# Third mixer in a new order: the convolution first, the state-space heads in pairs around a projection each, top-k beside the gates, four decay rows

## The chip, the cores and the metric

One core of a Trainium2 chip runs the whole program. The time is device microseconds from the start to the end of one execution. The engines are TensorE (PE, with its weight loads PEld), VectorE (DVE), ScalarE (ACT), GpSimd (POOL) and SyncE (SP), which issues most of the DMAs. They run beside each other, each through its own instructions in order, and meet through semaphores.

## The reference, cut to what matters

256 tokens of width 1024 pass through two blocks. The first has two layers with three kinds of attention. The second has one layer: a mixer (the third mixer of the program) and a mixture of 32 experts, of which each token uses four. All is float32. The change touches the third mixer alone:

```python
h = _rms(x, norm_mix[l]) * (1.0 + sc_m) + sh_m
q, kv_lat, q_i, k_i, w_i, z, xbc, dt_raw, gate_logits = _split(h @ w_in[l])
q = _rms(q, q_norm[l]);  k, v = split(_rms(kv_lat, kv_norm[l]) @ w_kv_up[l]);  k = _rms(k, k_norm[l])
k_i = _layernorm_2(k_i, ...)
y_attn = _dsa_attention(q, k, v, q_i, w_i, k_i, rel_bias) @ w_attn_o[l]
y_ssd = _mamba2_ssd(z, xbc, dt_raw, ...) @ w_ssm_o[l]
mixed = sigmoid(g_attn) * y_attn + sigmoid(g_ssd) * y_ssd
x = x + g_m * (mixed @ w_out[l])
```

`_dsa_attention` gives each query a score per key from 8 index heads (the sum over heads of w_i * relu(q_i k_i)), keeps the best 64 keys and runs softmax attention over these, in 8 heads. `_mamba2_ssd` is a causal convolution of width 4 over 1536 channels, a SiLU, and then 16 heads: for each, a matrix of decays exp(acum_i - acum_j), times the product of C and B (`cb`), times dt, is applied to the values x. The result plus d_skip * x is gated by SiLU(z) and normed.

## The kernel before

Every engine's program is written out by hand, one after the other, in the file; the order of the lines of an engine is the order of its work. Activations lie feature-major: tile `hT` holds 8 chunks of 128 features by 256 tokens.

**PE.** `features` (line 439) makes one "projection": two chunks of 128 output features, each 8 matmuls over the contraction, in one PSUM bank. `take` hands out seven banks in rotation; a bank can be taken again once its reader has freed it, so the take of the n-th bank waits for the reader of the (n-7)-th. `weights` waits for one of four ring slots of 2 MB; SP fills them group after group in the list `groups`, each when PE has finished with the group four before. The 16 state-space heads go through `A{h}` (line 815, the cumulative decay of a head, spread over the rows), DVE's `decay_in`, an exponential on ACT, DVE's `decay_out`, and `ssm_values` (lines 479 and 480). The decay rows have two buffers in the tile `sc2` (named sc in the rows). Four heads share a bank `yssm`, which DVE reads with the skip term (line 1631).

The order of the mixer before: projections of q, kv, index queries, index key and index weights (lines 728 and 734); conv inputs x0 to x2; time steps (line 747) and two gates; the norms of q, kv and index key; key/value projection; index heads; then the transposes of x, and the loop over 16 heads, with six projections in three places (behind the decay rows of heads 2, 7 and 12); four gate projections; the norm sum of y (line 457); scores t0 to t7; turning of the softmax weights (line 473) and their values; the attention output `ya`, the state-space output `ys`, the last product `wo`.

**DVE** does the convolution as four taps over twelve chunks (line 1586 and the one before) once all conv inputs are there, then the index sums, the key norm, the decay work, the gate by z, and then top-k: eight rounds of max and replace on each half, the mask, and the addition to the bias rows `bm`, followed by the y norm and the score rows. **ACT** reads projections out of PSUM in the order of PE, and does all exponentials, Silu, Sigmoid and norms.

**The expert stage** begins when the mixer's result is normed and routed. Per expert 12 MB come in: four ring slots (line 1086) and two slots of the down weights, each issued by SP when PE has used what was in the slot.

## Time and profile before

| | us |
|---|---|
| median of 3 runs (lowest, highest) | 1880.21 (1879.91, 1883.44) |
| the profiled execution's own time | 1882.82 |
| its span, first to last instruction | 1881.0 |
| PE matmuls busy in the span | 1648.2 (88%) |
| DVE busy | 392.8 (21%) |
| ACT busy | 300.3 (16%) |
| chain that ended last | PE 68%, DMA 17%, DVE 7%, ACT 4% |

The span is cut into 40 slices of 47 us. The third mixer lies in slices 11 to 19; there the row of PE reads 7 9 9 5 7 6 8 6 9, the row of PEclk 8 9 9 7 7 7 8 7 9. From slice 22 to 39 the DMA rate is 427 to 429 GB/s. A matmul of float32 is two passes in the trace, so its counts (x128) are twice the number of matmuls in the code. The granted clock is given as a share of 2.4 GHz: 1.00 is 2.4 GHz, 0.50 is 1.2 GHz.

### The profile page before, as it was taken

To read this page: it belongs to the slowest core of one execution; us is meant where nothing else is said; L and a number is where in the kernel's file an instruction comes from. 1 tells how busy PE (TensorE), PEld (TensorE's weight loads), DVE (VectorE), ACT (ScalarE), POOL (GpSimd) and SP (SyncE) were. 2 spreads that over 40 slices of the span, in tenths; PEclk is the share of its full clock that TensorE was granted. 3 is DMA by queue.
4 is the path that set the end of the run, shared out by engine and by line. 5 is a ranking of instruction groups with operands and counts; after the bars stand their busy time and mean duration, and the time that the engine had idled before them with its cause. 6 is when DMAs were issued, how large, how long until landed. Compare 5 with 4: busy or idle time off the path is not lost.

```text
span 1881.0 us, 19486 instructions
## 1 busy us (share of the span) xinstructions
PE 1648.2 (88%) x7938; PEld 969.1 (52%) x7938; DVE 392.8 (21%) x881; ACT 300.3 (16%) x587; POOL 2.8 (0%) x9
## 2 busy tenths in 40 slices
PE   3998799988799576869799999999999999999996
PEld 3786577857687465758633343333333333333342
DVE  2103411071101623721211111111111111111111
ACT  2013311151302401220200110110101001010010
POOL 0000000000000000000000000000000000000000
PEclk7998899999899777879799999999999999999998
DMA  7347534482233112203499999999999999999994
GB/s 251 133 125 227 187 106 155 143 313 74 79 114 134 45 45 90 90 31 149 148 402 427 428 429 429 428 429 428 428 429 429 429 428 429 428 428 429 429 428 202
DMA packets 86184, 515.04 MB, mean 274 GB/s; under 512 B 7000, under 2 KB 10776, under 8 KB 61560
## 3 DMA queue, kind: packets, MB, share of 16 engines
q1 hardware_dynamic: 82328, 513.43, 67.9%
q10 hardware_dynamic: 3632, 0.54, 0.2%
q8 instruction: 35, 0.57, 0.1%
q0 software_dynamic: 176, 0.39, 0.1%
q14 instruction: 13, 0.11, 0.0%
HBM read 511.20 MB, written 3.15 MB: 273 GB/s over the span
## 4 chain that ended last, share of the span: by engine, by line
PE 68%; DMA 17%; DVE 7%; ACT 4%; issue 2%; ACTq 1%; DVEq 0%; SPq 0%
PE psum L439 25%; PE psum L930 18%; DMA ring<-in_w_gu 15%; PE psum L999 8%; PE psum L903 3%; PE psum L448 3%; PE psum L479 2%; PE psum L913 2%; DMA ring<-in_w_ada 2%; PE psum L921 1%; DMA w_router<-in_w_router 1%; DVE sc L1405 1%; PE psum L496 1%; PE psum L815 1%; PE psum L480 1%
## 5 line engine op out<-in xcount | busy, mean ns | idle before, releaser
L930 PE MATMUL psum<-ring,hg 128*64 128x512 f32 x2048 | 458.6, 596 | 21.4 <-DMA ring<-in_w_gu 21.4
L439 PE MATMUL psum<-hT,ring 128*128 128x256 f32 x1504 | 342.4, 391 | 6.2 <-ACT hT L1190 6.2
L439 PEld LDWEIGHTS psum<-hT,ring 128*128 128x128 f32 x1504 | 296.0, 197 | 52.5 <-issue 9.9
L930 PEld LDWEIGHTS psum<-ring,hg 128*64 128x64 f32 x2048 | 139.2, 137 | 312.4 <-issue 267.7
L999 PE MATMUL psum<-w_down,hiddenT 128*64 128x512 f32 x1024 | 229.3, 600 | 28.2 <-ACT hiddenT L1365 25.2
L999 PEld LDWEIGHTS psum<-w_down,hiddenT 128*64 128x64 f32 x1024 | 74.9, 138 | 162.2 <-issue 162.2
L1767 DVE TENSOR_SCALAR gu<-psum 128x512 f32<-128x512 f32 x32 | 22.1, 692 | 529.2 <-PE psum L930 529.2
L1361 ACT ACTIVATE hidden<-gu 128x512 f32<-128x512 f32 x32 | 20.2, 630 | 316.2 <-DVE gu L1767 316.2
L439 PE MATMUL psum<-yT,ring 128*128 128x256 f32 x256 | 60.9, 403 | 9.3 <-DVE yT L1397 9.3
L903 PE MATMUL psum<-pick,h_tok 128*128 128x128 f32 x512 | 63.5, 284 | 2.9 <-DVE passes L1750 2.9
L903 PEld LDWEIGHTS psum<-pick,h_tok 128*128 128x128 f32 x512 | 60.5, 197 | 8.2 <-issue 8.2
L913 PE MATMUL psum<-putT,o_slot 64*128 64x256 f32 x512 | 63.9, 389 | 0.7 <-ACT o_slot L1368 0.7
L913 PEld LDWEIGHTS psum<-putT,o_slot 64*128 64x128 f32 x512 | 46.8, 186 | 31.0 <-issue 25.2
L439 PEld LDWEIGHTS psum<-yT,ring 128*128 128x128 f32 x256 | 52.1, 204 | 18.9 <-DVE yT L1397 11.0
L1368 ACT ACTIVATE o_slot<-psum 128x512 f32<-128x512 f32 x32 | 19.1, 597 | 237.7 <-PE psum L999 237.7
L448 PE MATMUL psum<-ring,hT 128*128 128x512 f32 (+2 forms) x192 | 56.3, 451 | 0.0
L1739 DVE COPY bias_row<-k_all 128x128 f32 (+1 forms) x32 | 7.2, 224 | 210.2 <-PE psum L937 210.1
L448 PEld LDWEIGHTS psum<-ring,hT 128*128 128x128 f32 x192 | 36.5, 190 | 18.0 <-issue 14.3
L479 PE MATMUL psum<-sc 128*64 128x256 f32 x32 | 15.6, 594 | 29.7 <-DVE sc L1405 29.7
L921 PE MATMUL psum<-b_gu,bias_row 64*128 64x512 f32 x128 | 36.1, 641 | 0.0
L1359 ACT ACTIVATE putT<-psum 128x256 f32<-128x256 f32 x32 | 12.3, 384 | 144.8 <-PE psum L937 144.8
L1182 ACT ACTIVATE wide<-xT 128x512 f32<-128x512 f32 x20 | 11.7, 625 | 141.4 <-DVE xT L1427 72.2
(348 smaller groups left out, 1283.8 us busy)
## 6 DMA issues: line engine op xcount, KB each, us to landing
ring<-in_w_gu SPq DMA_DIRECT2D x128, 2048.0 KB, 22.5
w_down<-in_w_dn SPq DMA_DIRECT2D x64, 2048.0 KB, 20.7
ring<-in_w_in SPq DMA_DIRECT2D x24, 2048.0 KB, 8.0
ring<-in_w_ada SPq DMA_DIRECT2D x12, 2048.0 KB, 10.6
ring<-in_w_out SPq DMA_DIRECT2D x6, 2048.0 KB, 9.9
ring<-in_w_in SPq DMA_DIRECT2D x2, 2064.0 KB, 7.8
ring<-in_w_ssm_o SPq DMA_DIRECT2D x2, 2048.0 KB, 7.8
ring<-in_w_in SPq DMA_DIRECT2D x1, 2112.0 KB, 8.1
```

The costliest lines, as they stand in the source:

```text
L439: mm = pe.matmul(bank[0:m, c * T:(c + 1) * T], w[:, k, c0 + c * P:c0 + c * P + m], src[:, k, :], start=(k == 0), stop=(k == k_n - 1))
L448: mm = pe.matmul(bank[:, 0:n], src[:, k, blk * P:(blk + 1) * P], w[:, k, c0:c0 + n], start=(k == 0), stop=(k == k_n - 1))
L479: pe.matmul(bank[rows, c * T:(c + 1) * T], v[:, 0, cols], wT[:, 0:T], start=True, stop=False)
L480: return pe.matmul(bank[rows, c * T + P:(c + 1) * T], v[:, 1, cols], wT[:, T:W3], start=False, stop=True)
L903: mm = pe.matmul(psum[:, 4 + part, j * P:j * P + width * CAP], h_tok[:, b, c * P:(c + 1) * P], pick[:, b, 0:width, :], start=(b == 0), sto ...
L913: mm = pe.matmul(psum[:, c // 2, c % 2 * T:(c % 2 + 1) * T], o_slot[r, i * P:(i + 1) * P], putT[r, side, :], start=False, stop=False, skip ...
L921: pe.matmul(psum[:, 4 + part, :], bias_row[r, side, :, :].rearrange("p h s -> p (h s)"), b_gu[r, :], start=True, stop=False, skip_group_ch ...
L930: mm = pe.matmul(psum[half * CAP:(half + 1) * CAP, 4 + part, :], hg[:, k, side, :], w[:, c0:c0 + 512], start=False, stop=(k == KC - 1), sk ...
L999: mm = pe.matmul(psum[half * CAP:(half + 1) * CAP, 7, :], hiddenT[:, i, j * CAP:(j + 1) * CAP], w_down[:, j, c0:c0 + 512], start=(k == 0), ...
L1361: act.activation(hidden[:, 0, :], gu[:, 0, :], ACT.Sigmoid, scale=1.702).then_inc(ev("g_sig"), 1)
L1368: act.activation(o_slot[:, :], psum[:, 7, :], ACT.Copy).then_inc(ev("o_slot"), 1)
L1767: dve.tensor_scalar(gu[:, 0, :], psum[:, 4, :], 7.0, None, ALU.min).then_inc(ev("g_in"), 1)
```

## The change

Nothing is computed otherwise; the third mixer's work is put in another order on every engine.

- The weight groups, and with them the projections, begin with the conv inputs, time steps and two gates. The convolution is done two chunks at a time on DVE, right behind each projection, with its SiLU on ACT.
- The loop over 16 heads becomes a loop over 8 pairs. In a pair PE issues both decay rows, one projection (q, q, kv, index queries twice, index key with index weights, z0, z1), then the values of the pair before. DVE does the two `decay_in`, a small norm (`aside`), the two `decay_out` of the pair before.
- The decay rows have four buffers, in the tile `idx`, instead of two in `sc2`.
- The index heads, the key/value projection and the score rows stand between the projections of z and of the gates; so DVE's top-k lies beside the gate projections. The key norm stands ahead of top-k, the y norm behind the scores.
- The state-space output comes ahead of the attention output, with the turning and the values of the attention between its four projections.
- SP issues the bias rows behind x2 instead of x0, and `ao` behind `so0` and `so1`.

```diff
-    decay = early[:, NB * D:NB * D + 2 * W3].rearrange("p (i n) -> p i n", i=2)
...
+    decay = idx
...
-    for name, a0, a1 in [("q2", 0, 512), ("kvqi", 512, 1024), ("qkwi", 1024, 1352),
-                         ("x0", 2376, 2888), ("x1", 2888, 3400), ("x2", 3400, 3912), ("dtg", 3912, 4440),
+    for name, a0, a1 in [("x0", 2376, 2888), ("x1", 2888, 3400), ("x2", 3400, 3912), ("dtg", 3912, 4440),
+                         ("q2", 0, 512), ("kvqi", 512, 1024), ("qkwi", 1024, 1352),
                          ("z0", 1352, 1864), ("z1", 1864, 2376),
                          ("g1", 4440, 4952), ("g2", 4952, 5464), ("g3", 5464, 5976)]:
-        if name == "z0":
+        if name == "g1":
             group("kvup", a["w_kv_up_2"][0], 0, 1024)
         group(name, a["w_in_2"][0], a0, a1)
-    group("ao", a["w_attn_o_2"][0], 0, 1024)
     for j in range(2):
         group(f"so{j}", a["w_ssm_o_2"][0], 512 * j, 512 * j + 512)
+    group("ao", a["w_attn_o_2"][0], 0, 1024)
...
-                              decay[:, h % 2, :], h % 2)
+                              decay[:, h % 4, :], h % 2)
...
-        for h in range(SH):
-
-            bank = take(f"A{h}")
-            for b in range(NB):
-                mm = pe.matmul(bank[:, b * P:(b + 1) * P], dta[:, b, h:h + 1].broadcast_to([P, P]), up,
-                               start=True, stop=True)
-            full(mm, f"A{h}")
-            if h % 5 == 2 and h // 5 < 3:
-
-                for i in range(2):
-                    project_aside(2 * (h // 5) + i)
-            if h >= 1:
-                ssm_values(h - 1)
-        ssm_values(SH - 1)
...
+        def project_aside(p):
+
+            if p < 2:
+                w = weights("q2")
+                features(f"q2.{p}", w, hT, 256 * p, 2)
+                if p:
+                    last_of("q2", "q2.1")
+            elif p < 4:
+                w = weights("kvqi")
+                features(("kvl", "qi0")[p - 2], w, hT, 256 * (p - 2), 2)
+                if p == 3:
+                    last_of("kvqi", "qi0")
+                    pe.wait_ge(ev("sq_q"), 1)
+                    for j in range(2):
+                        square_sums(j, "q2ms", slice(2 * j, 2 * j + 2))
+            elif p == 4:
+                features("qi1", weights("qkwi"), hT, 0, 2)
+                pe.wait_ge(ev("sq_kv"), 1)
+                sum_chunks("kvms", wide, [range(4, 6)], means[:, 2, :])
+            elif p == 5:
+                w = weights("qkwi")
+                bank = take("ki")
+                for half in range(2):
+                    for k in range(KC):
+                        mm = pe.matmul(bank[half * HEAD:(half + 1) * HEAD, 0:T], w[:, k, 256:320], hT[:, k, :],
+                                       start=(k == 0), stop=(k == KC - 1))
+                full(mm, "ki")
+                bank = take("wi")
+                for b in range(NB):
+                    for k in range(KC):
+                        mm = pe.matmul(bank[:, b * AH:(b + 1) * AH], hT[:, k, b * P:(b + 1) * P], w[:, k, 320:328],
+                                       start=(k == 0), stop=(k == KC - 1))
+                full(mm, "wi")
+                last_of("qkwi", "wi")
+            else:
+                features(f"z{p - 6}", weights("z0"), hT, 256 * (p - 6), 2)
+                if p == 6:
+                    read_out(pe, "ki")
+                    bank = take("kimean")
+                    mm = pe.matmul(bank[:, 0:T], K["half"][:, :], ki[:, :], start=True, stop=True)
+                    full(mm, "kimean")
+                else:
+                    last_of("z0", "z1")
+                    pe.wait_ge(ev("sq_ki"), 1)
+                    bank = take("kivar")
+                    mm = pe.matmul(bank[:, 0:T], K["half"][:, :], wide[:, 6, :], start=True, stop=True)
+                    full(mm, "kivar")
+        for p in range(SH // 2 + 1):
+            if p < SH // 2:
+                for h in (2 * p, 2 * p + 1):
+                    bank = take(f"A{h}")
+                    for b in range(NB):
+                        mm = pe.matmul(bank[:, b * P:(b + 1) * P], dta[:, b, h:h + 1].broadcast_to([P, P]), up,
+                                       start=True, stop=True)
+                    full(mm, f"A{h}")
+                project_aside(p)
+            if p == 1:
+                read_out(pe, "xt11")
+            if p >= 1:
+                for h in (2 * p - 2, 2 * p - 1):
+                    ssm_values(h)
+
+        w = weights("z1")
+        features("z2", w, hT, 0, 2)
+        pe.wait_ge(ev("ki"), 1)
...
+        for h in range(4):
+            index_rows(h)
+        features("z3", w, hT, 256, 2)
+        last_of("z1", "z3")
+        for h in range(4, AH):
+            index_rows(h)
+        w = weights("kvup")
+        pe.wait_ge(ev("kvl"), 2)
+        for j in range(2):
+            features(f"k2.{j}", w, kvl, 256 * j, 2)
+        for b in range(NB):
+            tokens(f"v2.{b}", w, kvl, b, 512, 512)
+        last_of("kvup", "v2.1")
+        w = weights("g1")
+        features("g2", w, hT, 0, 2)
+        pe.wait_ge(ev("sq_k"), 1)
+        for j in range(2):
+            square_sums(j, "k2ms", slice(2 * j, 2 * j + 2))
+        features("g3", w, hT, 256, 2)
+        last_of("g1", "g3")
+        w = weights("g2")
+        features("g4", w, hT, 0, 2)
+        pe.wait_ge(ev("qk2"), 2)
+        for h in range(4):
+            head_rows(f"t{h}", q2, h // 2, k2, h // 2, h % 2)
+        features("g5", w, hT, 256, 2)
+        last_of("g2", "g5")
+        for h in range(4, AH):
+            head_rows(f"t{h}", q2, h // 2, k2, h // 2, h % 2)
         pe.wait_ge(ev("sq_y"), 1)
         sum_chunks("yms", wide, [range(4), range(4, 8)], means[:, 3, :])
...
+        pe.wait_ge(ev("y_ssm"), 1)
+        for j in range(2):
+            w = weights(f"so{j}")
+            for i in range(2):
+                features(f"ys{2 * j + i}", w, yS, 256 * i, 2)
+                if (j, i) != (0, 0):
+                    h = 4 * j + 2 * i - 2
+                    if h > 0:
+                        value_2(h - 2)
+                        value_2(h - 1)
+                    turn_2(h)
+                    turn_2(h + 1)
+            last_of(f"so{j}", f"ys{2 * j + 1}")
+        value_2(4)
+        value_2(5)
+        turn_2(6)
+        turn_2(7)
+        value_2(6)
+        value_2(7)
...
-            if name == "x0":
+            if name == "x2":
...
+        for i in range(6):
+            read_out(dve, f"xbc{i}")
+            for k in range(4):
+                for j in range(2):
+                    c = 2 * i + j
+                    x = xbc[:, c, k:k + T]
+                    if k == 0:
+                        ins = dve.tensor_scalar(xbcs[:, c, :], x, vec("conv_w", c), None, ALU.mult)
+                    else:
+                        dve.wait_ge(ev("tap"), 6 * i + 2 * k - 1 + j)
+                        ins = dve.scalar_tensor_tensor(xbcs[:, c, :], x, vec("conv_w", 12 * k + c), xbcs[:, c, :],
+                                                       ALU.mult, ALU.add)
+                    ins.then_inc(ev("conv") if k == 3 else ev("tap"), 1)
...
+        def aside(p):
+
+            if p == 4:
+                dve.wait_ge(ev("rstd_q"), 2)
+                stt(flat(q2), flat(q2), vec("q_norm_2"), flat(wide[:, 0:4, :]), ALU.mult, ALU.mult, ev("qk2"))
+            if p == 5:
+                dve.wait_ge(ev("rstd_kv"), 1)
+                for c in range(2):
+                    stt(kvl[:, c, :], kvl[:, c, :], vec("kv_norm", c), stat[:, :], ALU.mult, ALU.mult, ev("kvl"))
+            if p == 7:
+                ch.free(dve.tensor_tensor(ki[:, :], ki[:, :], product(dve, "kimean")[:, 0:T], ALU.subtract), "kimean")
+                ch.after(dve.tensor_copy(sink[:, :], ki[:, 0:1]), ev("ki_centred"))
...
-            A, d = product(dve, f"A{h}"), decay[:, h % 2, :]
-            if h >= 2:
-                dve.wait_ge(*values_done[("ssm", h - 2)])
+            A, d = product(dve, f"A{h}"), decay[:, h % 4, :]
...
+        for p in range(SH // 2 + 1):
+            if p < SH // 2:
+                decay_in(2 * p)
+                decay_in(2 * p + 1)
+                aside(p)
+            if p >= 1:
+                decay_out(2 * p - 2)
+                decay_out(2 * p - 1)
...
+        dve.wait_ge(ev("rstd_k"), 2)
+        stt(flat(k2), flat(k2), vec("k_norm_2"), flat(wide[:, 0:4, :]), ALU.mult, ALU.mult, ev("qk2"))
```

How the instructions stand on PE in the loop. `dta` gives the decay rows, `hT,ring` is a projection, `sc` (before) and `idx` (after) with the values are a head's values. Before, from the decay rows of head 2 to those of head 4:

```order
L815 MATMUL psum<-k_all,dta 128x128 x2
L439 MATMUL psum<-hT,ring 128x256 x32
L479 MATMUL psum<-sc 64x256
L480 MATMUL psum<-sc 64x128
L815 MATMUL psum<-k_all,dta 128x128 x2
L479 MATMUL psum<-sc 64x256
L480 MATMUL psum<-sc 64x128
L815 MATMUL psum<-k_all,dta 128x128 x2
```

After, pairs 1 and 2 of the loop:

```order
L802 MATMUL psum<-k_all,dta 128x128 x4
L439 MATMUL psum<-hT,ring 128x256 x16
L479 MATMUL psum<-idx,sc 64x256
L480 MATMUL psum<-idx,sc 64x128
L479 MATMUL psum<-idx,sc 64x256
L480 MATMUL psum<-idx,sc 64x128
L802 MATMUL psum<-k_all,dta 128x128 x4
L439 MATMUL psum<-hT,ring 128x256 x16
```

Before, only three of the sixteen heads had projections (two at once) between decay rows and values; now every pair has one of 16 matmuls there.

On DVE around top-k, where `xbc<-xbc,zg` is the gate by z, `k<-k,vecs,wide` the key norm and `top` the first of the eight rounds. Before:

```order
L1631 SCALAR_TENSOR_TENSOR xbc<-xbcs,d_skip,psum 128x256 x2
L1397 TENSOR_TENSOR xbc<-xbc,zg 128x2048
L1397 TENSOR_TENSOR idx<-idx,k_all 128x384
L1657 COPY idx<-idx 128x384
L1661 MAX top<-idx 128x8
```

After:

```order
L1475 SCALAR_TENSOR_TENSOR idx<-idx,wi 128x256
L1467 TENSOR_TENSOR xbc<-xbc,zg 128x2048
L1475 SCALAR_TENSOR_TENSOR k<-k,vecs,wide 128x1024
L1467 TENSOR_TENSOR idx<-idx,k_all 128x384
L1739 COPY idx<-idx 128x384
L1743 MAX top<-idx 128x8
```

The index sums now stand directly ahead of the gate by z and of top-k, and the key norm has moved in between; before, the whole loop over the heads lay between the index sums and top-k.

## Rows read from the trace of the kernel before

**Rows 1.** Windows: us; busy us (instructions) of PE, PEld, DVE, ACT, POOL; clock; DMA
```profile
489.40:599.40 110.00, 109.99 (x513) 94.90 (x514) 2.40 (x11) 14.44 (x28) 0.00 (x0) 0.94 0.31 106
599.40:645.80 46.40, 24.77 (x102) 16.88 (x100) 30.42 (x76) 27.81 (x47) 0.00 (x0) 0.74 0.26 91
645.80:757.70 111.90, 82.13 (x321) 62.57 (x321) 35.59 (x102) 14.69 (x25) 0.00 (x0) 0.73 0.16 57
...
790.80:813.40 22.60, 4.59 (x34) 3.33 (x33) 12.95 (x23) 8.43 (x34) 0.00 (x0) 0.61 0.17 64
813.40:898.20 84.80, 82.43 (x377) 68.53 (x378) 15.64 (x32) 8.29 (x14) 0.00 (x0) 0.96 0.27 100
...
1234.00:1850.00 616.00, 568.57 (x2890) 225.85 (x2890) 86.40 (x185) 57.22 (x104) 0.00 (x0) 1.00 1.01 428
```

**Rows 2.** Waits of SP's queue from 900 us: total us, times, longest
```profile
SPq L1086 <- PE psum L930: 446.3, 124, 30.1
```

**Rows 3.** Timeline of SP: start, us, what is issued
```profile
938.76 11.81 SPq L1086 DMA_DIRECT2D ring<-in_w_gu  x4
```

**Rows 4.** Chain that ended last, at expert 0: start, us, what
```profile
934.98 3.58 PE psum L930 x16
```

**Rows 5.** Chain that ended last, third mixer: start, us, what
```profile
489.41 37.68 PE psum L439 x160
...
527.09 6.25 PE psum L728 x32
533.33 4.22 PE psum L734 x32
...
581.89 3.48 PE psum L747 x32
585.37 13.92 PE psum L439 x64
...
653.51 14.97 PE psum L439 x64
...
787.46 3.47 PE psum L457 x16
...
827.01 41.69 PE psum L439 x192
```

**Rows 6.** The same chain, small matmuls at full clock and the first turned weights
```profile
668.49 0.58 PE psum L479 x2
669.06 0.22 PE psum L480 x2
669.28 0.66 PE psum L815 x4
...
813.38 1.62 PE psum L473 x6
...
820.39 0.48 PE psum L473 x3
```

**Rows 7.** DVE by form, 643 to 790 us: busy, mean ns, idle before and its end
```profile
L1405 DVE SCALAR_TENSOR_TENSOR sc<-sc,dt,cbs 128x256 f32<-128x256 f32 x16 | 7.8, 485 | 0.6
...
L1405 DVE SCALAR_TENSOR_TENSOR sc<-psum,neg_acum,k_all 128x128 f32<-128x128 f32 x16 | 5.6, 351 | 57.1 <-PE psum L815 56.7
...
L1631 DVE SCALAR_TENSOR_TENSOR xbc<-xbcs,d_skip,psum 128x256 f32<-128x256 f32 x8 | 3.8, 481 | 17.4 <-PE psum L480 17.2
```

**Rows 8.** Timeline of PE: a head's values, and the idle time before
```profile
672.64 1.00 PE L479 MATMUL psum<-sc 128*64 128x256 f32 x2 [2.72 <-DVE sc L1405]
```

**Rows 9.** Timeline of DVE: top-k's first row, the bias add behind it, the scores
```profile
761.20 0.56 DVE L1397 TENSOR_TENSOR idx<-idx,k_all 128x384 f32<-128x384 f32 x1
...
780.75 3.36 DVE L1397 TENSOR_TENSOR bm<-bm,idx 128x3072 f32<-128x3072 f32 x1
...
796.57 3.52 DVE L1678 SCALAR_TENSOR_TENSOR sc<-psum,bm 128x384 f32<-128x384 f32 x6
```

**Rows 10.** Windows again: the stretch right behind the index weights
```profile
537.50:543.00 5.50, 5.50 (x14) 4.42 (x14) 0.00 (x0) 0.18 (x1) 0.00 (x0) 0.50 0.78 271
```

287 lines of the change are left out of this document (117 added, 170 removed).

## The prediction

> **What bounds the kernel now.** I read the windows view of the third mixer first, then the chain of waits, then the waits of SP's queue and of the engines, and the timelines of VectorE (DVE), ScalarE (ACT) and TensorE (PE) where the change moves work.
>
> The third mixer runs from 489.4 to 898.2 us, 408.8 us. From 489.4 to 599.4 PE is busy all the time, from 813.4 to 898.2 nearly. Between, it is busy 24.8 of 46.4 us, 82.1 of 111.9 and, ahead of the softmax weights, 4.6 of 22.6, at a granted clock of 0.74, 0.73 and 0.61 [rows 1]. The busy time there is itself long, because much of it was done at the lower of the two clock levels, 1.2 GHz (0.50), instead of 2.4 GHz. So the mixer is bound by chains between PE, DVE and ACT in the middle and by PE at both ends.
>
> Does the end move with the mixer? From 1234 to 1850 us the expert stage is bound by its weights: the 16 DMA engines are full (428 GB/s) [rows 1]. But this stream has its start from PE: SP's issues of expert weights waited 446.3 us for PE's expert matmuls [rows 2], and the second expert's first load left at 938.76 [rows 3], just when PE had used the first quarter of expert 0 (934.98 + 3.58) [rows 4]. All bytes behind that point are the same, and everything from 898.2 to 938.8 hangs on the mixer's last product. A microsecond gained in the mixer is therefore a microsecond at the end.
>
> **What PE has to do in the mixer.** The change takes nothing away from PE; it puts the same matmuls in another order. So I add up the work at the full clock.
> - A "projection" of two 128-feature chunks is 16 matmuls of 256 columns. Six take 41.69 us at clock 1.0, 6.95 each or 0.434 per matmul [rows 5]. There are 31 of them (q 2, kv and index queries 3, conv inputs 6, gates 8, z 4, ys 4, wo 4); the four half-size ones of the attention output and the key/value projection add 3. 34 x 6.95 = 236.3 us.
> - Index key 6.25, index weights 4.22, time steps 3.48 [rows 5]: 13.95 us.
> - Sums of squares: 3.47 for the state-space norm [rows 5]; four of 512 columns (2 x 0.434) and four of 256: 8.7 us in all.
> - Cumulative decay of a head (line 815) 0.66, its values (lines 479 and 480) 0.58 + 0.22 = 0.80, at full clock [rows 6]. Sixteen heads: 23.4 us.
> - Index rows and score rows, 8 heads each: 384 columns, 1.5 x 0.434 = 0.65. 10.4 us.
> - Turning the weights 8 x 0.48 (line 473) [rows 6] and 8 x 0.80 for the values: 10.2 us.
> - Sixteen transposes of x at 0.16 (a third of 0.48), two cb products at 0.65, three small ones: 4.0 us.
>
> Sum 307.0 us. To it come the clock's losses and the waits that remain.
>
> **Clock.** The mixer still starts slow after the norm: 5 projections took 37.68 us instead of 34.75 [rows 5], 2.9 us. In the window after the 8-column index weights PE was at 0.50 for 5.5 us without a pause [rows 10]; a matmul pass took 0.39 us there (14 in 5.5) against 0.22 at full clock, so about 2.7 us are lost. The index weights are now in pair 5 of the loop, with values and decay rows behind them; I charge 2.7 again. Together 5.6 us.
>
> **The convolution first.** DVE's taps were 48 in one piece, with PE idle behind them. Now they go chunk pair by chunk pair: about 3 us of DVE under each projection of 6.95, and ACT's read (0.6) and two Silu there too. The last chunk pair ends some 5 us after x2 while PE has 3.48 + 13.9 us of time steps and gates. The softplus chain hides there as well. Cost 0; without that cover 5 us, once.
>
> **The loop in pairs.** Before, a head between projections went through DVE, ACT, DVE and PE one after the other: PE waited 2.72 us for the decay [rows 8] and did its part at half clock, and the stretch of [rows 1], 111.9 us, less its 6 projections leaves 70.2 us for 16 heads, 4.4 each, where PE's own work at full clock is 1.46. DVE idled 57.1 us in total for line 815 and 17.4 for the values [rows 7]. Now PE issues both decay rows of a pair (1.3), a projection (6.95), then the values of the pair before (1.6): 9.9 us. DVE has, per pair, two decay_in (three operations of 0.35 and a one-column copy, about 1.35 with gaps), two decay_out (0.49 for 256 columns and about 0.35 for 128, 0.9 with gaps), every second pair the skip term (2 x 0.48) [rows 7], and for some the q, kv or index-key norm of 0.6 to 1.3: 4.5 to 6.6 us. DVE waits for the values' bank at the end of every second pair, so decay_in of the next starts about 1.1 us late; its decay_out must be there 8.3 us after PE's pair start and comes at about 5.6 (6.6 in pair 5). Four decay buffers make the wait for the values two pairs old. ACT's exponentials lie half a projection ahead. I charge no wait. If the cover failed, a pair would pay up to the old price of 2 x (4.4 - 1.46) = 5.9 us. The two copies of the index-key chain (kimean in pair 6, kivar in pair 7) have a projection between them for 1.2 us of DVE and ACT; cost 0.
>
> **Top-k beside the gates.** Let 0 be the loop's last value. PE: z2 6.95, four index heads 2.6, z3 6.95, four more 2.6, key/value 6.95, g2 6.95, two sums 1.7: 34.7. DVE's index sums are inside that. ACT does its two Ln/Exp pairs until about 36.6, DVE the key norm (1.28) until 38. Top-k and the bias add, from 761.20 to 784.11, take 22.9 us [rows 9]: 61. The first score (3.52 us for six, 0.59) frees its bank at 61.6. PE meanwhile does g3, g4 (13.9), t0 to t3 (2.6), g5 (6.95), t4, t5 (1.3) and reaches t6 at 59.5; seven banks rotate, and t6 wants that of t0. **PE waits 2.2 us.** Before, the same place cost 22.6 us with 4.6 busy [rows 1], as nothing else was left to do. Behind it, from the first score (796.57 [rows 9]) to the first weights turned (813.38 [rows 6]) it was 16.8 us: scores, maxima, exponentials, the sums' reciprocal. So these are ready at 61 + 16.8 = 77.8, and the y norm, which stands ahead of the reciprocal, before that. PE needs y at 80.3 (t6, t7, sums, g6, g7) and the weights at 94.2 (two ys projections later). Both are covered, by 2.5 us at the least and by 16; a top-k that is late by x costs x. Turning and values are interleaved with ys; two waits stay, for the last read of o2 (0.8) and for the mix of the last product (1.6). Waits together 4.6 us.
>
> **The queue of SP.** The bias rows are now issued behind x2, where SP waits for the last layer's h_ready; behind it stands dtg, needed 45 us later. Each later weight group has its slot freed 15 us or more before it is read, and a load lands in about 8 us. Cost 0. ACT loads its tables once less.
>
> **Sum.** 307.0 + 5.6 + 4.6 = 317.2 us in place of 408.8: 91.6 us less. The profiled execution took 1882.82 us (span 1881.0), so 1791.2; the median of the runs shown is 2.6 lower, 1880.21, which makes **1788.6, say 1789 us**.
>
> **Unknown costs, from both sides.** The row of a clock drop in the small matmuls of a pair or in the transposes ahead of the loop does not exist in this form. Lower end: no drop anywhere, not even behind the index weights, and no wait at t6: 5 us less, 1784. Upper end: one drop like that of [rows 10] per pair, 2.7 x 8 = 21.6 us, 1811. I take none, since within the old loop values and decay rows straight after a projection ran at full clock ([rows 6] are those) and since behind the 16-column time steps, 3.48 us long, two projections took 13.92 us, full clock [rows 5].
>
> The Trainium skill ("TensorE: Matmul & The Clock Gate", section "A second HAM failure mode: psum-queue depth-cycling") speaks against the change: a kernel that cycles through its PSUM banks can pause so often between groups that the clock goes back and forth. The case here cycles seven banks, with groups of 1.3, 6.95 and 1.6 us. By that rule the loop would lose its drop per pair (the rival below); by the rows it loses one.
>
> **Rivals.**
> 1. *The clock falls in most pairs.* For: it fell in [rows 10] while PE was busy without a pause. Against: the groups between projections are 2.9 us, those there 4.22 behind 6.25. 21.6 us: about 1810.
> 2. *A wait in the chains that I hid*: ACT serves reads and exponentials in one queue, and the Silu of z stands ahead of the key norm; or DVE's bank waits meet PE in the loop. 10 us (a late top-k of 7 and 0.4 per pair): about 1799.
> 3. *The end does not follow the mixer*, because the expert stream is bound by something before its start that doesn't move. Against: [rows 2 to 4]. Then 1880.
> 4. *Slower: PE works at 1.2 GHz for most of the mixer.* One mechanism: small groups and short waits keep the granted clock down over projections that had 1.0. With a share s of the time at half clock and a matmul 1.8 times as long there, 307 / (1 - 0.45 s) + 4.6. It decides from s = 0.54, about the 0.73 that the old loop shows [rows 1]. At a clock of 0.70 (s = 0.6): 425, so 1897. Against: in the old loop two projections behind a stretch at half clock took 14.97 us [rows 5], only 1.1 over full clock.
>
> **How the numbers follow.** My forecast (1784 to 1796) 0.55; rival 1 0.16; rival 2 0.22; rival 3 0.03; rival 4 0.03; the rest is a better clock than charged. The range takes in rivals 1 and 2: 1782 to 1812. What a measurement of this kernel can tell from no change is about 0.2%, 3.8 us. Faster 0.95, same 0.02, slower 0.03.
>
> **What would show it.** The mixer's last product should end near 806 us of the span in place of 898.2; PE busy over 95% from 489 to 806; a granted clock of 0.95 or more there; one PE wait of about 2 us for DVE's first score row; the pairs of the loop 10 us apart; DVE's first top-k instruction about 38 us behind the last head's values; and the same 428 GB/s at the end. I am wrong if PE waits for the decay in the loop, if a clock of 0.50 appears inside it more than once, or if the wait ahead of the scores is over 5 us.

## The result, and the profile after

The changed kernel takes 1779.49 us (median of 4 runs, 1777.62 to 1782.28); beside it the kernel before took 1881.83 (4 runs, 1879.91 to 1884.57). The ratio is 0.9456, 95% interval 0.9437 to 0.9475. The forecast was 1789, its range 1782 to 1812: the sign and the place were right, the gain was larger than forecast (102.3 us in place of 91.6), and the time lies 2.5 us below the range. The profiled execution took 1779.8 us, its span is 1777.7.

First the windows of the changed kernel, as in [rows 1]: stretch, then busy time and instructions of PE, PEld, DVE, ACT, POOL, then PE's granted clock, DMA share, GB/s. The first is the whole third mixer, the second the loop of head pairs.

```profile
487.60:794.30 306.70, 299.62 (x1487) 252.65 (x1488) 121.90 (x309) 81.39 (x153) 0.00 (x0) 0.97 0.31 111
554.20:633.60 79.40, 78.98 (x421) 64.69 (x420) 38.18 (x107) 19.64 (x36) 0.00 (x0) 0.96 0.24 81
...
612.00:617.50 5.50, 5.50 (x20) 4.75 (x20) 4.08 (x12) 1.04 (x2) 0.00 (x0) 0.60 0.97 365
...
690.00:702.00 12.00, 8.52 (x35) 6.82 (x34) 11.19 (x13) 2.75 (x4) 0.00 (x0) 0.86 0.48 176
...
900.00:1600.00 700.00, 654.36 (x3338) 261.37 (x3336) 100.03 (x218) 66.67 (x121) 0.00 (x0) 1.00 1.01 428
```

The mixer's projections begin at 487.65 and its last product is done at 794.32: 306.7 us in place of 408.8 (489.4 to 898.2, [rows 1]), 102.1 less. PE is busy 97.7% of it at a clock of 0.97. Behind it the two kernels need the same: 983.4 us to the end of the span here, 982.8 before. The expert stream still moves 428 GB/s.

SP's queue and the chain at expert 0 answer to [rows 2 to 4]: the wait in total, the first load of expert 1, and the PE piece that released it (830.98 + 3.58 = 834.56).

```profile
SPq L1135 <- PE psum L979: 447.4, 124, 29.9
```

```profile
834.76 8.40 SPq L1135 DMA_DIRECT2D ring<-in_w_gu  x3
```

```profile
830.98 3.58 PE psum L979 x16
```

Where did PE's 79.4 us in the loop go? The chain that ended last (start, us, what) shows one pair from values to values, then the decay rows and the projection of pair 6, right behind the index weights of pair 5, then the index rows of four heads. L439 is a projection, L479 and L480 are the values, L802 the decay rows.

```profile
570.79 6.91 PE psum L439 x32
577.70 0.59 PE psum L479 x4
578.29 0.22 PE psum L480 x4
578.51 1.09 PE psum L802 x8
579.60 6.91 PE psum L439 x32
...
611.64 2.01 PE psum L802 x8
613.65 8.34 PE psum L439 x32
...
640.70 0.43 PE psum L819 x4
641.13 0.43 PE psum L820 x4
641.57 0.32 PE psum L819 x4
641.88 0.43 PE psum L820 x4
```

A pair is 570.79 to 579.60, 8.80 us, without a gap. The values of **both** heads take 0.59 + 0.22 = 0.81 us, what one head took in [rows 6]. The index rows of four heads take 1.61 us, 0.40 each, where 384 columns alone would be 0.65. DVE's idle time for the decay rows is down from 57.1 us [rows 7] to 22.8, and now costs nothing, as PE does not wait for it:

```profile
L1475 DVE SCALAR_TENSOR_TENSOR idx<-psum,neg_acum,k_all 128x128 f32<-128x128 f32 x16 | 5.6, 351 | 22.8 <-PE psum L802 22.4
```

The waits of PE in the mixer (total us, times, longest); left out are one ahead of its first product, 0.8 us without a releaser and two of 0.2 for the skip terms. The timeline shows the largest, which stands where [rows 1] had 22.6 us with 4.6 busy, and the chain the sum of squares behind it:

```profile
PE psum L465 <- DVE sc L1755: 3.5, 1, 3.5
...
PE psum L439 <- DVE zg L1467: 1.6, 1, 1.6
...
PE psum L479 <- ACT probT L1182: 0.8, 2, 0.4
```

```profile
693.62 0.48 PE L465 MATMUL psum<-k,q 64*128 64x128 f32 x2 [3.48 <-DVE sc L1755]
```

```profile
695.22 5.21 PE psum L457 x16
```

There is no wait for a decay. One wait of 3.5 us for the first score is there, and the sum of squares behind it takes 5.21 us instead of 3.47 [rows 5], at a clock of 0.86 in its window.

### The profile page after: what moved, and what is told of

Its sections match the earlier page's. It is cut to its first block, busy times and chain, and to the rows that moved or that the text cites. A ratio compares the mean times of both kernels' runs of the same rounds, so it can differ in the third digit from the quotient of the medians.

```text
span 1777.7 us, 19486 instructions
## 1 busy us (share of the span) xinstructions
PE 1608.0 (90%) x7938; PEld 945.4 (53%) x7938; DVE 393.0 (22%) x881; ACT 299.6 (17%) x586; POOL 2.8 (0%) x9
## 4 chain that ended last, share of the span: by engine, by line
PE 70%; DMA 18%; DVE 6%; ACT 3%; issue 1%; ACTq 1%; SPq 0%; DVEq 0%
PE psum L439 25%; PE psum L979 19%; DMA ring<-in_w_gu 16%; PE psum L1048 9%; PE psum L952 4%; PE psum L448 3%; PE psum L962 2%; DMA ring<-in_w_ada 2%; PE psum L970 1%; DMA w_router<-in_w_router 1%; PE psum L479 1%; PE psum L496 1%; ACT hiddenT L1435 1%; ACT hg L1424 0%; PE psum L473 0%
## 5 line engine op out<-in xcount | busy, mean ns | idle before, releaser
L439 PE MATMUL psum<-hT,ring 128*128 128x256 f32 x1504 | 337.1, 386 | 6.4 <-ACT hT L1239 6.2
L439 PEld LDWEIGHTS psum<-hT,ring 128*128 128x128 f32 x1504 | 290.4, 194 | 52.0 <-issue 11.7
L439 PE MATMUL psum<-yT,ring 128*128 128x256 f32 x256 | 60.7, 403 | 9.3 <-DVE yT L1467 9.3
L439 PEld LDWEIGHTS psum<-yT,ring 128*128 128x128 f32 x256 | 52.0, 204 | 18.9 <-DVE yT L1467 11.0
L448 PE MATMUL psum<-ring,hT 128*128 128x512 f32 (+2 forms) x192 | 56.3, 451 | 0.0
L448 PEld LDWEIGHTS psum<-ring,hT 128*128 128x128 f32 x192 | 36.5, 190 | 18.0 <-issue 14.3
L1424 ACT ACTIVATE hg<-psum 128x512 f32<-128x512 f32 x32 | 19.1, 597 | 89.4 <-PE psum L952 89.4
L1858 DVE TENSOR_TENSOR hidden<-hidden 128x512 f32<-128x512 f32 x32 | 33.4, 1045 | 1.1
## 6 DMA issues: line engine op xcount, KB each, us to landing
ring<-in_w_ada SPq DMA_DIRECT2D x12, 2048.0 KB, 10.5
```

Source lines behind the costliest of these rows:

```text
L439: mm = pe.matmul(bank[0:m, c * T:(c + 1) * T], w[:, k, c0 + c * P:c0 + c * P + m], src[:, k, :], start=(k == 0), stop=(k == k_n - 1))
L448: mm = pe.matmul(bank[:, 0:n], src[:, k, blk * P:(blk + 1) * P], w[:, k, c0:c0 + n], start=(k == 0), stop=(k == k_n - 1))
L1424: act.activation(hg[:, 4 * part:4 * part + 4, 0:width, :], bank[:, :, 0:width, :], ACT.Copy)\
L1858: dve.tensor_tensor(hidden[:, 2, :].rearrange("s (i p) -> s p i", i=4), apart(hidden[:, 1, :]), apart(hidden[:, 0, :]), ALU.mult).then_inc ...
```

## Experiments

Twelve kernels in three series, each series on one chip beside 9 runs of the kernel before (1881.60 to 1881.75 in the median). "Mixer" is the stretch from the first projection to the last product, read from the chain that ended last: 306.7 us in the changed kernel, and in its second run below.

### Values of a pair apart

```diff
                     full(mm, f"A{h}")
+                    if p >= 2 and h == 2 * p:
+                        ssm_values(2 * p - 3)
                 project_aside(p)
...
-                for h in (2 * p - 2, 2 * p - 1):
-                    ssm_values(h)
+                ssm_values(2 * p - 2)
```

> The changed kernel with the two heads of a pair no longer neighbours when their values are computed: one decay row stands between them (the values of head 2p-3 come between the decay rows of heads 2p and 2p+1). The work is the same. Theory A: the two heads of a pair write different halves of the output rows, and PE does their values side by side when they follow each other: 0.81 us for both in the changed kernel's chain, where I had charged 0.80 for each. Apart, six or seven pairs pay up to 0.8 us more, the overlap with the decay row gives some back: mixer 3 to 6 us longer. Theory B: the values are only quick because nothing makes PE wait for them, and the 0.80 of the old row held some waiting: then no difference (under 1 us).

1785.41 us, ratio 0.9484 (0.9471 to 0.9497); mixer 313.3, 6.6 longer. Its chain:

```profile
571.55 6.91 PE psum L439 x32
578.46 0.58 PE psum L479 x2
579.03 0.22 PE psum L480 x2
579.25 0.64 PE psum L802 x4
...
581.33 6.91 PE psum L439 x32
```

Apart, each head costs 0.80 again, and the two decay rows 1.28 instead of 1.09; the pair takes 9.78 us instead of 8.80. No wait appears. The same instructions are dearer when the two heads are not neighbours.

### Neighbours on the same half

```diff
+        def in_order(h):
+            return h // 4 * 4 + (0, 2, 1, 3)[h % 4]
...
-            mm = apply_values(psum[:, banks[name][0], :], h // 2 % 2, x_tok, slice(h * HEAD, (h + 1) * HEAD),
-                              decay[:, h % 4, :], h % 2)
+            mm = apply_values(psum[:, banks[name][0], :], hh // 2 % 2, x_tok, slice(hh * HEAD, (hh + 1) * HEAD),
+                              decay[:, h % 4, :], hh % 2)
```

> The changed kernel with the state-space heads taken in the order 0, 2, 1, 3 of each four, on TensorE, VectorE and ScalarE alike: the two heads of a pair then write the same 64 partitions of their bank, where they wrote different ones. Number, shapes and order of the instructions are those of the changed kernel. Theory A (the values of two heads run side by side because they write different halves): the four products of a pair take 1.5 to 1.6 us instead of 0.81, the pair 9.5 to 9.6 instead of 8.80, and over 8 pairs the kernel is 5 to 6.5 us slower, 1784 to 1785.5. Theory B (the values are short when they stand together behind a projection, whatever they write, and the single heads' 0.80 us was a cost of going back and forth between shapes): the pair stays at 8.80 us and the time at 1778.5.

1783.14 us, ratio 0.9477 (0.9464 to 0.9490), in a series of its own; mixer 310.1, 3.4 longer. A pair's values in its chain:

```profile
578.49 0.58 PE psum L479 x2
579.07 0.22 PE psum L480 x2
579.28 0.43 PE psum L479 x2
579.72 0.22 PE psum L480 x2
```

The four pieces are 1.44 us (578.49 to 579.93) in place of 0.81, and the pair is 9.44 (571.58 to 581.02) in place of 8.80. The instructions stand in the same order, with the same shapes; only the place they write differs. In the changed kernel a pair writes the same columns of the bank in different 64 partitions, here neighbouring columns in the same 64. That is theory A: two heads run side by side when they write different halves. Of the 5.1 us that eight pairs would give, 1.4 came back in pair 6, whose projection took 6.91 here and 8.34 there; why the clock was back earlier is open.

The index rows are the same question with the rows *read* in place of the partitions written:

```diff
-        for h in range(4):
+        for h in (0, 2, 1, 3):
             index_rows(h)
...
-        for h in range(4, AH):
+        for h in (4, 6, 5, 7):
```

> On TensorE, the index score rows are issued in the order of heads 0, 2, 1, 3, then 4, 6, 5, 7, so that two neighbours read the same 64 rows of the array, where the changed kernel alternates between the lower and the upper 64. Theory A (two heads on different halves run side by side, and that is why four heads take 1.61 us where I had charged 0.65 each): the four heads take 2.0 to 2.6 us, 0.43 to 1 more per group of four. Theory B (their matmuls are only short, whatever half they read): 1.6 us per group as before. The time of the kernel moves by no more than 2 us either way, which this single look does not resolve; the rows of the chain decide.

A single run, 1782.23 us, so the rows decide and not the time; mixer 309.4. The first and the last piece of four heads in its chain:

```profile
640.53 0.41 PE psum L819 x2
...
642.36 0.43 PE psum L820 x2
```

From 640.53 to 642.79 they take 2.26 us in place of 1.61. In the order 0, 1, 2, 3 there are three neighbours on different halves, here one (2 and 1). Four heads alone would be 4 x 0.65 = 2.60; 2.60 - 1.61 is 0.33 for each of three, and 2.60 - 0.33 = 2.27 for one. So each pair of neighbours on different halves saves a third of a microsecond, half a head. Twice 0.65 is 1.3 of the 2.7 us that the mixer is longer; the wait for the first score is 3.5 us as before, and the rest lies behind it, where the last rows and the sum of squares (5.94) ran slower than in the changed kernel.

### Projections ahead of the loop

The eight projections of the loop, and what ACT and DVE do for them, stand ahead of it, so nothing lies between a pair's decay rows and its values.

```diff
+        for p in range(SH // 2):
+            project_aside(p)
+
         pe.wait_ge(ev("dta"), 1)
         bank = take("acum")
...
                     full(mm, f"A{h}")
-                project_aside(p)
```

> The changed kernel with the eight projections of the loop (q, kv, index queries, index key and weights, z0, z1) and their reads and norms moved ahead of the loop; pairs and four decay rows stay. Theory A (the projections beside the loop give the gain, since they cover DVE and ACT): the loop is bound by DVE, about 2.7 + 1.8 + 0.5 us a pair, some 5.2 us against the 1.9 us that PE needs: 8 x 3.3 = 26 us longer, and the projections ahead cost the same 62 us as before. Some more for the clock, which falls in the loop and must come back behind it (1 to 3 us). Theory B (pairs and four rows are what removes the old loop's chain, the projections' place matters little): under 10 us longer.

1819.08 us, ratio 0.9671 (0.9656 to 0.9685); the span is 39.2 us longer. One pair of its chain:

```profile
646.02 1.12 PE psum L479 x2
...
648.47 1.17 PE psum L805 x4
649.71 0.36 DVE idx L1477
...
652.93 0.36 DVE idx L1477
653.33 1.11 PE psum L479 x2
```

PE does the values and the first decay row at half clock, then DVE forms two exponents and the first decay, then PE again: 7.31 us a pair, where the changed kernel pays 8.80 - 6.91 = 1.89 beside its projection. So the cover is worth 5.4 us a pair, and that price holds the lower clock too (0.59 from 640 to 660 us). I had expected less for this run since I took DVE's work alone for the bound; but PE's decay rows stand behind its values, so PE and DVE take turns. The prediction's own price of a failed cover, 5.9, was the better one.

### Single heads

Two decay rows instead of four; each head's decay row, half a projection, then the values of the head before.

```diff
-                              decay[:, h % 4, :], h % 2)
+                              decay[:, h % 2, :], h % 2)
...
-            if h >= 4:
-                dve.wait_ge(*values_done[("ssm", h - 4)])
+            if h >= 2:
+                dve.wait_ge(*values_done[("ssm", h - 2)])
```

> The changed kernel with single heads instead of pairs, two decay rows instead of four, and half a projection (8 matmuls) beside each head; at head 8 the values come ahead of the half projection, which banks demand. Theory A: half a projection, 3.46 us, is long enough to cover decay_in and decay_out (2.3 us after the decay row), so the chain stays hidden; what is lost is the pairing of values and decay rows on PE (0.4 + 0.1 us a head, 6 to 8 us) and one wait of 2 us at head 8: 7 to 11 us longer. Theory B: pairs and four rows are needed to hide the chain: each head shows a wait of about 1 us or more, and the whole is 20 us or more longer.

1792.63 us, ratio 0.9523 (0.9509 to 0.9538); span 13.4 longer. A head of its chain (L448 is the projection, L489 the values' first piece; 0.22 of L490 and the decay row's 0.64 follow):

```profile
562.58 3.46 PE psum L448 x16
566.03 0.58 PE psum L489 x2
...
567.47 3.46 PE psum L448 x16
```

No wait: half a projection beside each head, 3.46 us, already hides the chain. A head takes 4.90, two 9.80, 1.0 more than a pair; over eight that is 8 of the 13. The rest are waits: 2.4 us at head 8, and 1.3 and 1.2 for the skip terms behind the values of heads 7 and 11, where the changed kernel has 0.2 each. Behind the first two the clock fell and cost another 3 us (5.67 us for half a projection); about as much was saved behind the index weights, where it did not fall (see below). So what the pair has over single heads is for the larger part not a better cover but that its two heads are neighbours on PE.

### Convolution in one piece

```diff
-        for i in range(6):
-            read_out(dve, f"xbc{i}")
-            for k in range(4):
-                for j in range(2):
-                    c = 2 * i + j
+        read_out(dve, "xbc5")
+        for k in range(4):
+            for c in range(12):
```

ACT's Silus stand behind its last read accordingly.

> The changed kernel with the convolution in one piece again, behind the last conv input: 48 taps on DVE, 17.6 us, then the chain of the time steps. The prediction said that the new place costs nothing since it is covered. Theory A: DVE is done with the taps at 532.8 + 17.6 = 550.4, the softplus chain takes some 4 us more, so PE, which is ready at 549.6 for it, waits until about 555 and loses some clock: 5 to 9 us longer. Theory B: the order of time steps and taps gives PE enough to do: under 1 us.

1788.83 us, ratio 0.9514 (0.9500 to 0.9529); mixer 316.1, 9.4 longer. PE's first piece behind the convolution, and the transposes:

```profile
555.10 1.04 PE psum L727 x4
...
556.56 3.49 PE psum L735 x16
```

PE idles 6.6 us for dta, and the sums and transposes behind it then take 1.04 and 3.49 us where the changed kernel has 0.35 and 1.79: 2.4 us of lower clock, 3.0 with the products ahead of the loop. I had priced the missing cover at 5 us in the prediction; it is 9. (Behind the index weights this kernel lost 1.6 us less than the changed one: 7.23 us for the projection there in place of 8.34, and 1.18 for the values in place of 1.49. No run says why.)

### Half the top-k ahead of the gate

```diff
-        dve.wait_ge(ev("z_gate"), 1)
-        tt(yS[:, :, :], yS[:, :, :], zg[:, :, :], ALU.mult, ev("y_gated"))
-        dve.wait_ge(ev("rstd_k"), 2)
-        stt(flat(k2), flat(k2), vec("k_norm_2"), flat(wide[:, 0:4, :]), ALU.mult, ALU.mult, ev("qk2"))
...
         for cols, q in PARTS:
+            if q:
+                dve.wait_ge(ev("z_gate"), 1)
+                tt(yS[:, :, :], yS[:, :, :], zg[:, :, :], ALU.mult, ev("y_gated"))
+                dve.wait_ge(ev("rstd_k"), 2)
+                stt(flat(k2), flat(k2), vec("k_norm_2"), flat(wide[:, 0:4, :]), ALU.mult, ALU.mult, ev("qk2"))
             work, best = idx[:, 1, cols], top8[:, q, :]
```

The changed kernel once more, in the same series:

> The changed kernel once more, in the same series as the three edits of it that follow, so that their times can be set beside it. Every theory: 1779.5 us within 2.

1778.50 us (1777.65 to 1779.46), ratio 0.9454 (0.9441 to 0.9467), mixer 306.7.

> On VectorE, the addition of the causal mask, the copy and the first half of the top-k stand ahead of the product with the z gate and the normalization of the keys, which now stand between the two halves. Nothing else changes. In the changed kernel TensorE idles 3.5 us at head 3's score row, because its bank frees only when VectorE has cleared it behind both halves, and the sum of squares behind that wait takes 5.21 us where it took 3.47 before. Theory A (the wait is a plain chain on VectorE, and the clock fall behind it is the wait's): the score banks are cleared about 11 us earlier, the wait goes, the sum of squares is back at 3.5 us, and the mixer and the kernel end 5 us earlier (3.5 + 1.7), at about 1774. Theory B (the normalized keys are then what comes late: the score rows wait for them instead, which are written 11.4 us later): the keys are needed at about 683 us, and the half takes 11.4 us from 670, so they would be ready at about 684: a wait of 1 to 3 us at the first score row, and the time is 1776 to 1779. Theory C (the fall of the clock has nothing to do with the wait): the wait goes, the sum keeps its 5.2 us, 1776.

1771.99 us (1769.15 to 1773.63), ratio 0.9416 (0.9403 to 0.9429); once more in the next series 1771.06 (1769.60 to 1774.22), ratio 0.9415 (0.9402 to 0.9428):

> The kernel with the first half of the top-k ahead of the gate once more, as the base of the two edits of the index weights that follow in this series: 1772 us within 2, by every theory.

The mixer takes 300.8 us, 5.9 less. The chain where the wait was:

```profile
691.84 0.43 PE psum L466 x4
692.27 3.65 PE psum L457 x16
```

The wait is gone, the sum of squares is back at 3.65, and no new wait for the keys comes in: theory A. The expectation names head 3; by the rotation of seven banks the row that waited in the changed kernel is that of t6, the seventh bank taken behind that of t0. This version beats both kernels. Its two profiles also need 1.9 and 2.2 us less behind the mixer than the changed kernel's in the same series (980.9 and 980.6 against 982.8), and begin the mixer 2.4 and 1.2 us later, which the edit does not explain. Behind the mixer the largest piece is this: the first down projection of expert 0 took 9.48 us in the changed kernel, at the lower clock, and 7.09 here, as all later ones do. In both kernels and in the profiles of the ten other edits and reruns the clock was lower there: 8.42 to 9.78 us for that piece, behind much the same short waits of the routing (2.0 and 2.9 us in the changed kernel, 2.3 and 2.6 in the two of this version); no run says why it was not in the two of this version.

### The clock behind the index weights

Block 0 of the 8-column products ahead of the index key:

```diff
+                for b in range(NB):
+                    for k in range(KC):
+                        mm = pe.matmul(wi_bank[:, b * AH:(b + 1) * AH], hT[:, k, b * P:(b + 1) * P],
+                                       w[:, k, 320:328], start=(k == 0), stop=(k == KC - 1))
+                    if b == 0:
+                        bank = take("ki")
...
```

> On TensorE, the sixteen 8-column products of the index weights for block 0 stand ahead of the index key's products, those for block 1 behind them, where the changed kernel has all 32 in a row. The changed kernel shows the clock at half speed for about 5.5 us from 606 us on, and the work behind the row (decay rows 1.06, values 2.01, a projection 8.34 instead of 6.91) loses 3.0 us. Theory A (the run of narrow products is what the clock falls for): in two pieces of 1.9 us each between full work the clock stays at 1.00, and the kernel is up to 3 us faster, 1776 to 1778. Theory B (it falls after any narrow products, or for another reason): the clock falls as before or twice, 1779 to 1783.

1778.74 us, ratio 0.9456 (0.9444 to 0.9469): no change. The two rows of 16 passes and the key between them:

```profile
598.69 1.92 PE psum L773 x16
600.61 7.91 PE psum L779 x32
608.52 1.88 PE psum L773 x16
```

The clock now fell twice (0.72 from 600 to 606 us, 0.74 from 612 to 618): the key (7.91 in place of 6.29) pays what the values and decay rows behind the second row no longer pay. Next, on top of the early half of the top-k, the narrow products one by one between those of the key, and then all but two of them left out:

```diff
                         mm = pe.matmul(bank[half * HEAD:(half + 1) * HEAD, 0:T], w[:, k, 256:320], hT[:, k, :],
                                        start=(k == 0), stop=(k == KC - 1))
+                        mm = pe.matmul(wi_bank[:, half * AH:(half + 1) * AH], hT[:, k, half * P:(half + 1) * P],
+                                       w[:, k, 320:328], start=(k == 0), stop=(k == KC - 1))
```

> Beside the early half of the top-k, the 32 products of the index weights stand one by one between the 32 of the index key, so that no two narrow products are neighbours. When they stood in two pieces of 16 the clock still fell, behind the first piece of 1.9 us, and nothing was won. Theory A (a run of narrow products is what the clock falls for): alternating, it stays at 1.00, and the kernel is up to 3 us faster than the one without, about 1769; the whole group takes at least 6.29 + 3.87 = 10.2 us as before, less if a narrow one hides beside a wide one. Theory B (the share of narrow products over a stretch is what counts, not that they are neighbours): the clock falls in the group or behind it, which then takes up to 13 us, and the time is 1771 to 1775.

> Beside the early half of the top-k, of the 32 products of the index weights only the first of each block is left (the index weights are then sums over the first 128 of 1024 features; everything else is computed). Their row takes 3.87 us, at 0.12 each. Theory A (the narrow products make the clock fall): the row shrinks to 0.24 us, the half speed behind it goes, and the kernel is 3.6 + 3.0 = 6.6 us faster, about 1765.5. Theory B (the clock falls there for another reason, such as the index key's 64-column products ahead): the row goes and the fall stays, 3.6 us faster at most, 1768 to 1769.

These two texts count passes: what they call 32 products are 16 matmuls, 32 passes in the trace, and the last edit leaves 2 of the 16: it leaves out the sums over the other 896 of 1024 features.

Interleaved: 1775.24 us, ratio 0.9439 (0.9426 to 0.9452), mixer 301.9, 1.1 longer than without; the other 3 us lie behind the mixer, where the first down projection took 9.78 us. With two products: 1768.15, ratio 0.9399 (0.9386 to 0.9412), mixer 294.4, 6.4 shorter. Windows of the interleaved group, and of the stretch behind the two products:

```profile
598.70:613.30 14.60, 14.44 (x67) 7.91 (x68) 5.19 (x15) 1.28 (x3) 0.00 (x0) 1.00 0.00 1
```

```profile
606.00:618.00 12.00, 11.79 (x72) 9.83 (x72) 5.45 (x16) 2.10 (x5) 0.00 (x0) 1.00 0.51 175
```

Both hold a clock of 1.00 where the changed kernel shows 0.60 from 612 to 617.5 (its windows above). So the row of narrow products, during which PE counts as busy, has a part in the fall, here as in [rows 10]: taken out or pulled apart, it leaves the clock at 1.00. But the row alone does not make the clock fall. In the single heads' kernel the same 32 passes stand in one row (L792); ahead of them, where the changed kernel has the key, are a head's values and a decay row (L815):

```profile
617.57 0.64 PE psum L815 x4
618.21 3.47 PE psum L792 x32
621.68 0.58 PE psum L489 x2
```

The row takes 3.47 us instead of 3.88, the values behind it are at full speed, and the granted clock is 1.00 from 618 to 624. The 32 passes of 16 columns of the time steps, 3.48 us at 532.23, are followed by full clock as well (13.91 us for two projections). So what the fall needs beside the row, what stands ahead of it or the moment at which it comes, stays open. Alternating also changes two things at once, the neighbours of a narrow product and the time over which the narrow ones are spread.

Alternating saves the 3.0 us but makes the group 14.3 us instead of 6.29 + 3.88: one wide and one narrow product take 0.90 instead of 0.64. If all of that is put on the narrow one, a pass of it costs 0.25 instead of 0.12. In the other edit the two products that stay take 0.54 us in place of 3.88: 3.3 for the row and 3.0 for the clock, 6.4 measured in the mixer. 3.5 of it were lost again behind the mixer, most of it at the routing and expert 0, which ran at the lower clock (first gather 6.54 against 5.32, first down projection 8.42 against 7.09), so the kernel is only 2.9 us faster.

## What the prediction had right, and the step that failed

**The bound and the end.** Right. The mixer's microseconds arrive at the end one for one: 102.1 in the mixer, 102.3 in the medians. Rival 3 is out.

**No wait in the loop.** Right: 79.0 of 79.4 us busy. The run with the projections ahead shows what the cover is worth (5.4 us a pair, 40.6 in the mixer; 5.9 was the prediction's bound), the single heads that half a projection beside each head does as well. Rival 2 is out.

**The clock.** Rival 1 asked for a fall in most pairs, rival 4 for most of the mixer at 1.2 GHz. In the loop it fell once, behind the index weights of pair 5, as charged, and cost 3.0 us there (2.7 forecast; the rows it was worked out from, 14 passes at 0.22 in 5.5 us, give 2.4). That it fell at all was not bound to happen: in the single heads' kernel it did not. By the rule that the prediction cited from the Trainium skill ("TensorE: Matmul & The Clock Gate", section "A second HAM failure mode: psum-queue depth-cycling") this loop was a candidate for falls between its groups; seven banks cycle through groups of 1.09, 6.91 and 0.81 us, and the trace shows full-clock durations in each. The rule's pauses are not there: PE idles 0.4 us in 79.4. It did not apply. Not charged was the fall behind the wait for the first score, 1.74 us.

**The step that failed: PE's work in small groups.** The prediction charged each head by itself: "its values (lines 479 and 480) 0.58 + 0.22 = 0.80", sixteen times, and 0.65 for each index and score row, on the ground that "the change takes nothing away from PE; it puts the same matmuls in another order". The order takes something away. In [rows 6] a head stood alone; in the changed kernel two are neighbours. Where these write or read different halves, they run side by side; where they do not (decay rows, turned weights), only the first of the two pays for following another kind of work. The terms, forecast and as the chain shows them (at full clock; the slow ones are in the clock's row):

| term | forecast us | measured us |
|---|---|---|
| projections, 34 | 236.3 | 236 |
| index key, index weights, time steps | 13.95 | 13.65 |
| sums of squares | 8.7 | 8.6 |
| values of 16 state-space heads | 12.8 | 6.5 |
| decay rows of 16 heads | 10.6 | 8.3 |
| index and score rows | 10.4 | 6.4 |
| turning the weights, values of 8 heads | 10.2 | 7.3 |
| ahead of the loop | 4.0 | 3.7 |
| clock: start, index weights, behind the first score | 5.6 | 7.8 |
| waits | 4.6 | 7.0 |
| sum | 317.2 | 305.2; the mixer is 306.7, and 1.5 are in no row |

The four rows of heads are 44.0 forecast and 28.5 measured. Against these 15.5 stand 2.2 more of clock, 2.4 more of waits and the 1.5 in no row; with 1 less in the other rows that makes the 10.5 us by which the mixer came out below the forecast. The values apart (+0.98 a pair) and the pairs on one half (+0.64 a pair) show this on the chip for the first row, the index rows on one half (+0.65 per four heads) for the third. For the last row it is only read from the trace (at 735.62 and 736.42, 0.81 for the values of two heads and 0.81 for turning two, forecast 1.60 and 0.96). For the decay rows, which use all partitions, two neighbours cost 1.09 behind values and 0.89 behind a projection, one alone 0.64 [rows 6 had 0.66]; so a first one after another kind of work is dearer than a second. Why, no run here says.

**The waits.** Forecast 2.2 us at the first score, measured 3.5. DVE's 22.9 us for the top-k and the bias were right. Counted from the loop's last value, DVE frees the bank at 60.0 us (61.6 forecast), but PE, whose index and score rows are shorter than charged, stands at t6 at 56.5 (59.5 forecast). The sign given for the start of the top-k, 38 us behind the last head's values, was 36.5. The early half of the top-k takes both away, and the mixer is 5.9 us shorter.

**The range.** Its low end allowed for no drop and no wait, 5 us below the forecast, and for nothing in the work itself. A lower bound of the head terms was missing: I took one row's duration as both ends, although that row stood in another neighbourhood.

## What to carry to other kernels

When a change puts small matmuls side by side, do not price them one by one from a trace in which they stood alone: two that write different halves of the partitions, or read different halves of the rows, may cost little more than one, so order heads to alternate halves. The chain of a head over DVE and ACT was hidden by half a projection (3.46 us) beside it, and what a cover is worth shows only without it. A wait of PE can cost more than itself: 3.5 us of it cost 1.7 of lower clock behind it here, 6.6 us cost 3.0. A row of very narrow matmuls can cost the clock too, although PE counts as busy; whether it does is to be read from the durations behind it, since the same row did in one order and not in another.

## What the hardware showed that I had not expected

- Two neighbouring heads on different halves of the output partitions: 0.81 us for both; on the same half 1.44; with a decay row between 0.80 each. On different halves of the rows read, each neighbour saves 0.33 us of 0.65.
- Sixteen 8-column products in a row (32 passes, 3.88 us, PE busy throughout) and a granted clock of 0.60 behind them; two rows of half the length do it as well (0.72 in 600 to 606 us); alternating with 256-column ones the clock stays at 1.00, but a wide and a narrow product take 0.90 us instead of 0.64. In the single heads' kernel the whole row stood behind a decay row, and the clock stayed at 1.00.
- A change of a few us ahead of the expert stage moved the time of single pieces far behind it by up to 2.7 us, since the clock falls there in most kernels and by different amounts: the first down projection of expert 0 took 7.09 us in one version and 8.42 to 9.78 in the others. Differences of 3 us in this kernel are to be read in the stage, not in the total.
